# A hybrid block and a conformer block on one core: the moving activations read in turns between the two halves of a tile

## What is computed

```python
# first block: one input projection, three branches, gates, output
h = rms_norm(x, pre_g)
a_u, a_v, a_g, b_x, b_g, x_q, x_g, gate_logits = split(h @ w_in)      # 7 x 1024, then 3 x 2048
y_a = spatial_gating(a_u, a_v, ...) * silu(a_g)
y_b = s5_branch(b_x, ...) * silu(b_g)                                  # scan over the tokens, GLU
y_x = memory_cross_attention(x_q, rms_norm(mem), xa_wk, xa_wv) * silu(x_g)
merged = sum over n of sigmoid(gate_logits[n]) * (ys[n] @ w_branch[n])
x = x + rms_norm(merged @ w_out, post_g)
# second block: convolution module and MLP
u = rms_norm(x) @ w_pw1 + b_pw1;  u = a * sigmoid(gate)                # a, gate: the halves of u
u = depthwise convolution of 31 taps over the tokens
x = x + silu(layer_norm(u)) @ w_pw2 + b_pw2
x = x + square(relu(rms_norm(x) @ w_up)) @ w_down                      # 2048 -> 8192 -> 2048
return rms_norm(x)
```

## Time and profile before

| | us |
|---|---|
| median of 3 | 1963.95 |
| profiled execution | 1964.09 |
| its span | 1962.1 |
| TensorE busy | 1941.2 (99%), 11210 matmuls |
| VectorE busy | 1498.2 (76%) |
| ScalarE busy | 965.1 (49%) |
| GpSimd busy | 416.3 (21%) |
| weights and inputs moved | 377.45 MB, 192 GB/s |

### The profile page before, as it was taken

The page is one execution under the profiler, slowest core; times in us unless marked ns, Lnnn a source line. Parts: engine busy times, 40 slices in busy tenths (PEclk is TensorE's granted clock), DMA queues, the critical chain, the costliest instruction groups (busy, mean ns, idle before and its releaser), DMA issues.

```text
span 1962.1 us, 28447 instructions
## 1 busy us (share of the span) xinstructions
PE 1941.2 (99%) x11210; PEld 1707.4 (87%) x11210; DVE 1498.2 (76%) x2243; ACT 965.1 (49%) x1346; POOL 416.3 (21%) x310
## 2 busy tenths in 40 slices
PE   9999999999999999999999999999999999999998
PEld 8888888888887788888899988888888888888887
DVE  7977888878899976778899996776567557656765
ACT  6555444434444355557643476554444444444444
POOL 0000234433366620000486743000000000000000
PEclk9999999999999999999999999999999999999999
DMA  9765665555666566666556656666666666666664
GB/s 330 233 188 181 193 187 171 169 168 176 185 189 183 175 191 190 201 218 187 159 173 212 189 170 187 185 200 190 203 196 187 202 202 186 193 204 194 191 202 153
DMA packets 105974, 377.45 MB, mean 192 GB/s; under 512 B 11889, under 2 KB 14449, under 8 KB 105713
## 3 DMA queue, kind: packets, MB, share of 16 engines
q1 hardware_dynamic: 105552, 375.10, 62.7%
q10 hardware_dynamic: 288, 0.53, 0.1%
HBM read 372.90 MB, written 2.69 MB: 191 GB/s over the span
## 4 chain that ended last, share of the span: by engine, by line
PE 80%; DVE 15%; ACT 2%; issue 2%; DMA 1%; POOL 0%; DVEq 0%; ACTq 0%
PE bank L2009 23%; PE bank L2020 12%; PE bank L2076 7%; PE bank L2074 7%; PE bank L2075 7%; DVE wl L1132 6%; PE bank L2057 3%; PE bank L2059 3%; PE bank L2058 3%; PE bank L2091 3%; PE bank L2092 3%; PE bank L2093 3%; ACT wh L730 1%; PE bank L2275 1%; DVE wsc L1516 1%
## 5 line engine op out<-in xcount | busy, mean ns | idle before, releaser
L1132 DVE TENSOR_TENSOR wl<-raw,wh 128x1024 fp32r<-128x1024 f32 x608 | 758.6, 1253 | 345.0 <-ACT wh L730 344.1
L730 ACT ACTIVATE wh<-raw 128x1024 fp32r<-128x1024 f32 x680 | 711.9, 1054 | 591.9 <-PE bank L2076 206.6
L2009 PE MATMUL bank<-Hr,wh 128*128 128x512 f32 x1536 | 370.8, 392 | 0.1
L2009 PEld LDWEIGHTS bank<-Hr,wh 128*128 128x128 f32 x1536 | 281.5, 188 | 55.2 <-issue 0.7
L661 POOL TENSOR_TENSOR wl<-raw,wh 128x1024 fp32r<-128x1024 f32 x72 | 174.3, 2430 | 310.1 <-DVE small L1707 241.9
L2074 PE MATMUL bank<-wh,Yr 128*128 128x512 f32 x560 | 212.3, 379 | 0.0
L2075 PE MATMUL bank<-wl,Yr 128*128 128x512 f32 x560 | 212.2, 379 | 0.0
L2076 PE MATMUL bank<-wh,Yr 128*128 128x512 f32 x560 | 212.2, 379 | 0.0
L2020 PEld LDWEIGHTS bank<-Hr,wl 128*128 128x128 f32 x1536 | 197.4, 191 | 8.8 <-issue 1.1
L2009 PE MATMUL bank<-Yr,wh 128*128 128x512 f32 x832 | 201.7, 392 | 0.3 <-DVE gate_b L1202 0.3
L2020 PE MATMUL bank<-Hr,wl 128*128 128x256 f32 x1536 | 200.5, 283 | 0.0
(11 more groups left out here) (381 smaller groups left out, 2772.3 us busy)
## 6 DMA issues: line engine op xcount, KB each, us to landing
raw<-in_w_up SPq DMA_DIRECT2D x128, 512.0 KB, 3.6
raw<-in_w_dn SPq DMA_DIRECT2D x128, 512.0 KB, 3.5
raw<-in_w_g SPq DMA_DIRECT2D x96, 512.0 KB, 3.5
raw<-in_w_p SPq DMA_DIRECT2D x80, 512.0 KB, 3.7
raw<-in_w_b SPq DMA_DIRECT2D x48, 512.0 KB, 3.6
raw<-in_w_out SPq DMA_DIRECT2D x32, 512.0 KB, 3.5
raw<-in_w_q SPq DMA_DIRECT2D x16, 512.0 KB, 4.4
raw<-in_w_av SPq DMA_DIRECT2D x16, 512.0 KB, 3.6
```

Source lines behind the costliest of these rows:

```text
L730: e.activation(wh[:, c % WN, :], raw[:, c % RAW, :], ACT.Copy).then_inc(s_hi, 1)
L1132: e.tensor_tensor(wl[:, c % RAW, :], raw[:, c % RAW, :], wh[:, c % WN, :].bitcast(F32), ALU.subtract).then_inc(s_low_v, 1)
L2009: ins = e.matmul(dst, wh[:, s, kk * 128:kk * 128 + 128], pair.both[:, :, k, :], start=i == 0 and kk == 0, stop=i == j.nch - 1 and kk == 7, ...
```

## The change

Every matmul that has activations as its moving operand reads the 256 tokens in turns between the tile's two halves: token 0, 128, 1, 129, ... So column 2u + s of the bank holds token 128s + u. Whoever reads such a bank reads every second column and writes (or combines with) one half of the tokens, then the other. `woven` is renamed `in_turns`; the weights' products are as before. Number and order of instructions, waits and transfers stay. The diff, without the places that repeat:

```diff
+    def tokens(turned):
+        return turned.rearrange("p (u s) -> p s u", s=2)
+    def halves(row):
+        return row.rearrange("p (s u) -> p s u", s=2)
...
         def half(j, dst, **kw):
             w.wait_ge(s_mm, j.end)
-            e.activation(dst, bank[j.banks[0]][:, T:2 * T], ACT.Copy, **kw).then_inc(s_half, 1)
+            e.activation(halves(dst), tokens(bank[j.banks[0]][:, T:2 * T]), ACT.Copy, **kw).then_inc(s_half, 1)
...
-                e.activation(kept(j), of(j), ACT.Identity, bias=cv("bpw1", t)).then_inc(s_evac, 1)
+                e.activation(halves(kept(j)), tokens(of(j)), ACT.Identity, bias=cv("bpw1", t)).then_inc(s_evac, 1)
...
-                e.activation(of(j) if t >= 14 else kept(j), of(j), ACT.Tanh, scale=0.5,
+                e.activation(tokens(of(j)) if t >= 14 else halves(kept(j)), tokens(of(j)), ACT.Tanh, scale=0.5,
                              bias=hb[:, t:t + 1]).then_inc(s_evac, 1)
...
         def add_half(j, dst):
             w.wait_ge(s_half, j.half)
-            e.tensor_tensor(dst, dst, bank[j.banks[0]][:, 0:T], ALU.add).then_inc(s_comb, 1)
+            e.tensor_tensor(halves(dst), halves(dst), tokens(bank[j.banks[0]][:, 0:T]), ALU.add).then_inc(s_comb, 1)
...
-                e.scalar_tensor_tensor(pad[:, 15:271], of(j) if t >= 14 else kept(j), 1.0, kept(AT["a", t]), ALU.add,
+                gate = tokens(of(j)) if t >= 14 else halves(kept(j))
+                e.scalar_tensor_tensor(halves(pad[:, 15:271]), gate, 1.0, halves(kept(AT["a", t])), ALU.add,
                                        ALU.mult).then_inc(s_pad, 1)
...
-        def woven(row):
+        def in_turns(row):
             return row.rearrange("p (s n) -> p n s", s=2)
+        def by_turns(rows):
+            return rows.rearrange("p h (s u) -> p h u s", s=2)
...
-            dst = bank[j.banks[0]].rearrange("p (h t) -> p h t", h=2)
+            dst = bank[j.banks[0]].rearrange("p (h u s) -> p h u s", h=2, s=2)
...
-                ins = e.matmul(dst, wh[:, s, kk * 128:kk * 128 + 128], pair.both[:, :, k, :],
+                ins = e.matmul(dst, wh[:, s, kk * 128:kk * 128 + 128], by_turns(pair.both[:, :, k, :]),
...
-                ins = e.matmul(dst, wl[:, r, kk * 128:kk * 128 + 128], pair.hi[:, k, :],
+                ins = e.matmul(dst, wl[:, r, kk * 128:kk * 128 + 128], in_turns(pair.hi[:, k, :]),
...
-                    e.matmul(dst[:, 0:T], lh, pair.hi[:, k, :], start=first_part and kk == 0, stop=False)
-                    e.matmul(dst[:, 0:T], lh, pair.lo[:, k, :], start=False, stop=False)
-                    ins = e.matmul(dst[:, 0:T], ll, pair.hi[:, k, :], start=False, stop=last_part and kk == 7)
+                    e.matmul(dst[:, 0:T], lh, in_turns(pair.hi[:, k, :]), start=first_part and kk == 0, stop=False)
+                    e.matmul(dst[:, 0:T], lh, in_turns(pair.lo[:, k, :]), start=False, stop=False)
+                    ins = e.matmul(dst[:, 0:T], ll, in_turns(pair.hi[:, k, :]), start=False, stop=last_part and kk == 7)
```

More of the change, by code:

```diff
@@ L1218, in evac @@
                 w.wait_ge(s_half, j.half)
-                e.scalar_tensor_tensor(qT[:, t, :], bk[:, 0:T], 1.0 / 16, qT[:, t, :], ALU.mult,
-                                       ALU.add).then_inc(s_comb, 1)
+                e.scalar_tensor_tensor(halves(qT[:, t, :]), tokens(bk[:, 0:T]), 1.0 / 16, halves(qT[:, t, :]),
+                                       ALU.mult, ALU.add).then_inc(s_comb, 1)
                 times_norm(j)
@@ L1300, in evac @@
                 done(w, j)
-                e.scalar_tensor_tensor(Xf[:, t, :], bk[:, 0:T], cv("bpw2", t), Xf[:, t, :], ALU.add,
+                x = halves(Xf[:, t, :])
+                e.scalar_tensor_tensor(x, tokens(bk[:, 0:T]), cv("bpw2", t), x, ALU.add,
                                        ALU.add).then_inc(s_v, w.own())
                 w.wait_ge(s_v, w.n)
-                e.tensor_tensor(Xf[:, t, :], Xf[:, t, :], bk[:, T:2 * T], ALU.add).then_inc(s_comb, 1)
+                e.tensor_tensor(x, x, tokens(bk[:, T:2 * T]), ALU.add).then_inc(s_comb, 1)
                 w.wait_ge(s_h2h, t + 1)
@@ L2051, in chunk @@
                         w.wait_ge(s_act, n0 + k // per + 1)
-                        rh = woven(wh[:, s, kk * 512:kk * 512 + 512])
-                        rl = woven(wl[:, r, kk * 512:kk * 512 + 512])
+                        rh = in_turns(wh[:, s, kk * 512:kk * 512 + 512])
+                        rl = in_turns(wl[:, r, kk * 512:kk * 512 + 512])
                         xh = pair.hi[:, k, h * 128:h * 128 + 128]
@@ L2125, in first_tiles @@
                     o = (kk * 4 + m) * 128
-                    e.matmul(bank[j.banks[0]].rearrange("p (h t) -> p h t", h=2), wh[:, s, o:o + 128],
-                             pair.both[:, :, k, :], start=k == 0, stop=k == 15, skip_group_check=True)
+                    e.matmul(bank[j.banks[0]].rearrange("p (h u s) -> p h u s", h=2, s=2), wh[:, s, o:o + 128],
+                             by_turns(pair.both[:, :, k, :]), start=k == 0, stop=k == 15, skip_group_check=True)
             low_there(c)
@@ L2132, in first_tiles @@
                     o = (kk * 4 + m) * 128
-                    ins = e.matmul(bank[j.banks[0]][:, 0:T], wl[:, r, o:o + 128], pair.hi[:, k, :], start=False,
+                    ins = e.matmul(bank[j.banks[0]][:, 0:T], wl[:, r, o:o + 128], in_turns(pair.hi[:, k, :]), start=False,
                                    stop=k == 15, skip_group_check=True)
@@ L2152, in chunk_for_all @@
                     if apart:
-                        e.matmul(of(j), lh, pair.hi[:, k, :], start=a, stop=False, skip_group_check=True)
-                        e.matmul(of(j), ll, pair.hi[:, k, :], start=False, stop=False, skip_group_check=True)
+                        e.matmul(of(j), lh, in_turns(pair.hi[:, k, :]), start=a, stop=False, skip_group_check=True)
+                        e.matmul(of(j), ll, in_turns(pair.hi[:, k, :]), start=False, stop=False, skip_group_check=True)
                         continue
@@ L2157, in chunk_for_all @@
                         both = bank[j.banks[0]]
-                        e.matmul(both.rearrange("p (h t) -> p h t", h=2), lh, pair.both[:, :, k, :], start=a, stop=z,
+                        e.matmul(both.rearrange("p (h u s) -> p h u s", h=2, s=2), lh, by_turns(pair.both[:, :, k, :]), start=a, stop=z,
                                  skip_group_check=True)
-                        ins = e.matmul(both[:, 0:T], ll, pair.hi[:, k, :], start=False, stop=z, skip_group_check=True)
+                        ins = e.matmul(both[:, 0:T], ll, in_turns(pair.hi[:, k, :]), start=False, stop=z, skip_group_check=True)
                         if z and j.tells:
@@ L2168, in chunk_for_all @@
                         dst = bank[j.banks[0]][:, T:2 * T] if j.kind == "W" else of(j)
-                        ins = e.matmul(dst, wh[:, s, o:o + 128], pair.lo[:, k, :], start=False, stop=k == 15,
+                        ins = e.matmul(dst, wh[:, s, o:o + 128], in_turns(pair.lo[:, k, :]), start=False, stop=k == 15,
                                        skip_group_check=True)
```

## The result

The changed kernel takes 1913.79 us in the median (1912.75 to 1914.17, four runs) against 1963.97 before: a ratio of 0.9743, 95% interval 0.9726 to 0.976, or 50.2 us less. The forecast was 1908.

A forecast was written before the change was run, and what follows sets the result against it. The prediction took TensorE's matmuls, busy 99% of the span, as the bound: 32.1 + 40.8 = 72.9 us saved, less 16 taken back, gains 57; 1963.95 - 57 = 1907, stated as 1908, range 1892 to 1940.

The forecast's parts named there:

- TensorE sets the end, and products over activations pay 13 ns too much each: Whole kernel: TensorE, busy 99%, sets the end; products over activations pay 13 to 16 ns over their columns, `dn` 2 to 3.
- 512 columns at 216 ns: The 2472 products of 512 columns over activations: 216 ns in place of 229, saving 32.1 us.
- 256 columns at 110 ns: The 4080 products of 256 columns over activations: 110 ns in place of 120, saving 40.8 us.
- Two reads in each other's way: TensorE's excess per product: the next stationary tile's load and the moving read get in each other's way; no fixed instruction price.
- What the rest takes back: 16 us: Stretches where another engine or DMA is nearly full: 9.4 + 1.5 + 1 + 3 = 14.9 lost, said 16 us.
- The start: First 28.90 us, DMA share 0.91: faster products wait for weights, 3 us lost with the next stretch.
- The convolution: 980.70 to 1166.00: of 13.4 us that its 1344 products give back, 4 kept and 9.4 lost to VectorE.
- VectorE leaves at most 7.2: In the convolution VectorE is busy 178.1 of 185.3 us, so at most 7.2 us can be gained.
- Readers free: ScalarE and VectorE reading banks with a step of two: 0 ns extra, upper bound 262 ns a read.
- B: Rival: only one product width gains, 1935 us with only the 512s or 1936 with only the 256s; chance 0.18.
- C: Rival: `dn` is fast because its weights move and activations are stationary, not by its walk; 1964 us, chance 0.10.
- D: Rival: slower, two alternating runs meet the stationary load worse; 240 ns per 512 columns, 1991 us, chance 0.07.

The follow-up runs named there:

- e1: The changed kernel with only the 512-column products in turns, the 256-column products read in order: 1940.61 us.
- e2: The changed kernel with only the 256-column products in turns, the 512-column products read in order: 1936.83 us.
- e4: The changed kernel with each low product loading and multiplying only 64 of the 128 stationary columns: 1911.30 us.
- e5: The kernel before the change with each low product loading and multiplying only 64 of the 128 stationary columns: 1952.92 us.
- e3: The changed kernel with no product in turns, ScalarE and VectorE still reading the banks with a step of two: 1964.42 us.
- w4: The changed kernel with all products over activations walking four runs of 64 tokens in turns: 2187.2 us.
- w64: The changed kernel with all products over activations walking with a step of four words (0, 4, 8, ...): 2994.1 us.
- w128: The changed kernel with all products over activations walking with a step of two words (0, 2, 4, ...): 2952.1 us.
- e9: The changed kernel with VectorE adding the low half on only 2 of 256 columns in stages au, ag and xg: 1910.61 us.
- e12: The changed kernel with the 256-column products in two runs of 64 words at a time, the 512s as in the change: 1914.21 us.
- e11: The changed kernel with the attention's pieces four chunks later (ATT = 116): 1916.84 us.

## Why the prediction was right

**TensorE sets the end, and products over activations pay 13 ns too much each.** The second half is right, by e1 and e2 as well as by the earlier trace rows. The first half is right for most of the span and not for all: it was taken from the busy share of 99%, and the chain of the same page puts 15% on VectorE.

**512 columns at 216 ns.** Right to the nanosecond. The third dimension and the 128 words don't matter.

**256 columns at 110 ns.** The term that was mis-sized: 112, so 8 and not 10 ns, 8 us less. I had taken from the earlier trace rows that a tile can be exchanged in 88 ns. The pace of the transposes doesn't carry over to these loads; why isn't shown. e4 shows 109 with a tile half as wide. The Trainium skill's formula (TensorE: Matmul & The Clock Gate, section "Wait — 56ns, not 53.3ns?"), 109.2 by the estimate, agrees with e4's 109 and not with the change's 112. (By that estimate the prediction's sum would have been 3.8 us larger, not 3.)

**Two reads in each other's way.** I had read this from the earlier trace rows. It stays an argument: e5 shows that 13 ns become 8 with a tile half as wide, which fits it, but doesn't tell the load from the product's own width. What two runs in turns do to avoid the cost isn't shown by a trace.

**What the rest takes back: 16 us.** 14.5 were taken (64.7 - 50.2), but from other places. The start lost 1.3 of its 2.6 and not 3. The convolution lost less than 1 where I said 9.4. The failed step there is "VectorE leaves at most 7.2", from its 178.1 busy us of 185.3: busy was read as work. The multiply into the padded row, L1287 (L1296 after), is the witness, before and after:

```profile
L1287 DVE SCALAR_TENSOR_TENSOR upad<-scrB,scrB 128x256 f32<-128x256 f32 x10 | 16.3, 1629 | 2.8 <-ACT scrB L845 2.8
L1287 DVE SCALAR_TENSOR_TENSOR wide<-scrB,scrB 128x256 f32<-128x256 f32 x4 | 9.5, 2367 | 1.1 <-ACT scrB L845 1.1
```

```profile
L1296 DVE SCALAR_TENSOR_TENSOR upad<-scrB,scrB 128x256 f32<-128x256 f32 x10 | 13.1, 1310 | 1.3 <-ACT scrB L853 1.2
L1296 DVE SCALAR_TENSOR_TENSOR wide<-scrB,scrB 128x256 f32<-128x256 f32 x4 | 7.2, 1811 | 0.0
```

The same 256 columns take 420 ns elsewhere, so most of 1629 and 2367 ns is standing with the instruction open. What it stands for can be seen beside GpSimd's subtractions, here in the kernel before:

```profile
1005.72 2.40 POOL L661 TENSOR_TENSOR wl<-raw,wh 128x1024 fp32r<-128x1024 f32 x1 [0.44 <-ACT wh L730]
1006.03 2.37 DVE L1287 SCALAR_TENSOR_TENSOR upad<-scrB,scrB 128x256 f32<-128x256 f32 x1 [0.75 <-ACT scrB L845]
```

Of the 14, the three that meet no instruction of GpSimd take 413 to 427 ns; each of the other eleven ends 0.28 or 0.29 us after the L661 that runs beside it has ended. The two L1287 that read one operand from a bank take 417 and 418 ns, one of them with L661 open. So VectorE stands until GpSimd's instruction is through, for about 20 of the 25.8 us that the 14 are busy: this part of its time isn't work, and it can shrink. With the change these 14 take 5.5 us less, and the convolution's VectorE time falls from 178.1 to 170.9. That VectorE would be the bound there was right even so: in chunks 340 to 401 the chain lay on TensorE before (189.1 of 190.8 us) and lies on VectorE after (152.6 of 181.4). It only had more room than its busy time showed.

In place of the convolution, the scan's stretch (chunks 80 to 223) took 7.7 us. The sum has no term for it. Over the whole stretch VectorE's share is 86%, which looks harmless; but a window inside it has VectorE full, and I had it before me when I made the sum and left it out:

```profile
553.90:657.80 103.90, 99.82 (x497) 82.98 (x496) 103.76 (x124) 43.37 (x54) 71.34 (x64) 1.00 0.61 183
```

It holds no products over activations itself, but what is gained just ahead of it has to pass through it. The rest of the 14.5 is spread: 1.6 us at `glu` and `bg` (chunks 252 to 283), 1.3 from there to the grouped `w_p1` chunks, and less in each of the other stretches. The two errors, 8.6 us and 7.7 us, cancel; the total of 16 was right by luck. What is left of the miss (1907 by the sum, 1914 measured) is the 256s' term, 8.2 us, less the 1.5 us by which 16 was too much.

**Readers free.** Right, e3.

**Rivals.** B falls with e1 and e2, C with the measurement, D with 216 ns. But D's idea was sound in a form that I hadn't written: another walk of the same family (w4, w64, w128) costs 220 to 1030 us. The Trainium skill's note on cachelines (SBUF — State Buffer, section "Door 1: The DMA port swizzle") would let fp32 step by up to four words for free. Measured, a step of two costs 230 ns in place of 120, and two runs in turns, where each read crosses a line, are the best walk of all; the measurement decides.

## What to carry to other kernels

Measure a matmul by the distance of starts, and compare it with its columns over the clock: if a product in this type pays 13 ns and others 3, look at how the moving operand walks. Two contiguous runs read in turns are worth trying wherever the order of the columns is free (here 6% of a 512, 7% of a 256, and free for the readers); steps and more than two runs cost far more than they could save. Before counting what arrives, follow the chain that ended last stretch by stretch: where it lies on another engine, nothing arrives, also where TensorE is busy 99% and the other 86%. And don't take an engine's busy time for its work when an instruction in it is far longer than its twins; see what the other engines run beside it.

## What was not expected of the hardware

- A step of two or four words in a moving operand of this type: 230 and 233 ns for 256 columns, 2.1 times the price in turns; four runs in turns 143. All at the full granted clock (0.999 in each of these runs).
- The half clock after one wait of 3.8 us in a kernel that is otherwise 98% busy: 0.50 in the window of the next 2.5 us, and some 1.5 us of it lost. It follows the same wait in e1, e4, e9 and e12, and in e11 the wait for L1210; in e2 and e5, where TensorE is idle for 2.85 and 2.43 us at this place, the clock stays at 1.00.
- VectorE's L1287 with both operands outside the banks is open for up to 2.7 us in place of 0.42 where GpSimd's L661 runs beside it, and ends 0.28 us after that one.
- A step of 2, 4, 64 or 128 columns in a bank costs ScalarE and VectorE nothing that is seen: VectorE's L1189 took 413 ns in the change, 415 in w4 and 414 in w64 and w128, against 415 read in order; ScalarE's L752 365 to 367 ns in all of them, against 366.
